# Two mixers of a second block rearranged: queries and keys of retention turned during the projection, retention's units first in the stream, and VectorE adding up the scores of the key selection

## The reference

```
x = x + 0.5 * swiglu(rmsnorm(x), ...)                 # ffn 1
p_a, p_b, p_c = split(rmsnorm(x) @ w_in)              # 1280, 1096 and 1024 columns
x = x + concat([rwkv7(p_a), dsa(p_b), retention(p_c)]) @ w_out
x = x + 0.5 * swiglu(rmsnorm(x), ...)                 # ffn 2
```

```
# rwkv7 (6 heads of 64): w = -softplus(-(w0 + tanh(w_lo) @ w2)) - 0.5; a = sigmoid(a0 + a_lo @ a2); g = sigmoid(g_lo) @ g2
#   decay = exp(-exp(w)); the recurrence uses products of decays within chunks of 64 steps; then a norm per head, times g
# dsa: score[q, s] = sum over 8 heads of iw[q, h] * relu(iq[q, h] . ik[s]); hidden where s > q
#   the 128 best keys of each query are selected; 6 heads of softmax attention on the latent c over the selected keys
# retention (4 heads of 64):
qh, kh = rotate(q), rotate(k)        # rotate: [z1*cos - z2*sin, z1*sin + z2*cos], z1 and z2 the halves of a head
y = (qh @ kh^T * decay(query - key)) @ v;  y = y * rsqrt(mean(y*y) + eps);  out = silu(g) * y
```

## Time and profile before

| | us |
|---|---|
| median of 3 runs | 4016.59 (4015.89 to 4021.63) |
| the profiled execution | 4007.51 |
| its span | 4005.7 |
| TensorE busy | 3738.7 (93%) |
| VectorE busy | 2057.2 (51%) |
| ScalarE busy | 1394.1 (35%) |
| GpSimd busy | 99.6 (2%) |

### The profile page before, as it was taken

How to read it: one execution, slowest core, us unless ns; L and a number is a source line. 1 busy time by engine, 2 the same in 40 slices (tenths; PEclk the granted TensorE clock), 3 DMA queues, 4 the chain that set the end, 5 groups by cost and what they waited for, 6 DMA issues and landing times. The chain is left out here.

```text
span 4005.7 us, 62023 instructions
## 1 busy us (share of the span) xinstructions
PE 3738.7 (93%) x26656; PEld 3221.2 (80%) x26656; DVE 2057.2 (51%) x3299; ACT 1394.1 (35%) x2153; POOL 99.6 (2%) x107
## 2 busy tenths in 40 slices
PE   8989998899889997999997799999999997799998
PEld 8989998788789996888876568888888875658886
DVE  6756654344366635443357554444443347655443
ACT  6534332455343323232225233223232225333321
POOL 0000000000000000000003000000000003100000
PEclk9999999999899998999987899999999997989999
DMA  3222232222122232333310013233233310012332
GB/s 137 68 85 85 90 94 65 71 64 65 48 75 89 89 88 72 96 97 97 96 45 2 22 58 100 95 94 101 95 98 96 96 56 2 23 48 95 100 92 76
DMA packets 87424, 307.03 MB, mean 77 GB/s; under 512 B 9696, under 2 KB 9824, under 8 KB 86896
## 3 DMA queue, kind: packets, MB, share of 16 engines
q1 hardware_dynamic: 87152, 303.08, 24.0%
HBM read 300.91 MB, written 2.13 MB: 76 GB/s over the span
## 5 line engine op out<-in xcount | busy, mean ns | idle before, releaser
L602 DVE TENSOR_TENSOR two_w_lo<-two_raw,two_w_hi 128x1024 fp32r<-128x1024 f32 (+1 forms) x344 | 412.7, 1200 | 848.3 <-ACT two_w_hi L593 845.3
L617 PE MATMUL psum<-two_x_hi,two_w_hi 128*128 128x512 f32 x1856 | 726.0, 391 | 28.4 <-DVE two_w_lo L602 28.4
L617 PE MATMUL psum<-two_x_lo,two_w_hi 128*128 128x512 f32 x1856 | 723.3, 390 | 0.0
L617 PE MATMUL psum<-two_x_hi,two_w_lo 128*128 128x512 f32 x1856 | 723.2, 390 | 0.0
L593 ACT CAST two_w_hi<-two_raw 128x1024 fp32r<-128x1024 f32 (+1 forms) x344 | 352.6, 1026 | 893.1 <-PE psum L617 888.2
L617 PEld LDWEIGHTS psum<-two_x_hi,two_w_hi 128*128 128x128 f32 x1856 | 349.1, 188 | 103.0 <-DVE two_w_lo L602 29.1
L1394 PE MATMUL psum<-one_x_hi,one_w_hi 128*128 128x264 f32 x1408 | 402.1, 286 | 23.1 <-DVE one_x_lo L1538 21.1
L617 PEld LDWEIGHTS psum<-two_x_lo,two_w_hi 128*128 128x128 f32 x1856 | 349.1, 188 | 74.0 <-issue 1.4
L617 PEld LDWEIGHTS psum<-two_x_hi,two_w_lo 128*128 128x128 f32 x1856 | 349.1, 188 | 72.3
L1394 PE MATMUL psum<-one_x_lo,one_w_hi 128*128 128x264 f32 x1408 | 401.0, 285 | 0.0
L1394 PE MATMUL psum<-one_x_hi,one_w_lo 128*128 128x264 f32 x1408 | 400.6, 285 | 0.0
(11 more groups left out here) (411 smaller groups left out, 6594.1 us busy)
## 6 DMA issues: line engine op xcount, KB each, us to landing
two_raw<-in_swi_in SPq DMA_DIRECT2D x176, 512.0 KB, 3.7
one_raw<-in_ffn_in SPq DMA_DIRECT2D x88, 512.0 KB, 3.6
two_raw<-in_swi_out SPq DMA_DIRECT2D x64, 448.0 KB, 3.3
two_raw<-in_mix_in SPq DMA_DIRECT2D x56, 512.0 KB, 3.7
one_raw<-in_attn_w SPq DMA_DIRECT2D x32, 512.0 KB, 3.8
two_raw<-in_swi_out SPq DMA_DIRECT2D x32, 512.0 KB, 3.5
one_raw<-in_ffn_out SPq DMA_DIRECT2D x32, 448.0 KB, 3.3
one_raw<-in_lru_w SPq DMA_DIRECT2D x24, 512.0 KB, 3.6
```

What stands on the lines that cost most here:

```text
L602: self.nc.vector.tensor_tensor(self.m.ws.lo[:, u % self.SLOTS, w], self.m.raw[:, u % self.RAW, w], self.m.ws.hi[:, u % self.SLOTS, w].bitc ...
L617: last = self.nc.tensor.matmul(self.m.ps[:, bank, :], a[:, u % self.SLOTS, w], b[:, k0 + k, :], start=(start and k == 0 and q == 0), stop= ...
```

## The change

- Projection: the sine (with its sign) and cosine tables are loaded into `m.keys` by one more DMA on SP's queue, ahead of the projection's first unit. At units 17 to 20 ScalarE copies one tile of retention's queries or keys with the 32-partition quarters exchanged, four copies a tile. At units 19 to 22 VectorE multiplies that copy by sine, the tile by cosine, and adds.
- Preparation: VectorE adds the scores up, with the head's weight in one instruction each; ScalarE keeps only relu, GpSimd sets the sums to zero and hides later keys beforehand. Tanh becomes a sigmoid with a VectorE instruction behind it. The constant of the log decay goes into the exponentials' scale, and the exponential of the previous step's sum is read from the other one, shifted by a step. Twelve of the 24 scores are placed among the tiles, the first four of them ahead of all, and the sums of squares go behind the third low-rank product. The other twelve scores are added four at a time after each tile of the last pass.
- The mixers' end: no turning. The stream has retention's first six units in front, inside the head; then ten pairs; then 14 key-selection units. RWKV's outputs are made at key-selection units 4, 6 and 8, the norm of retention's output at 11, 13 and 15, and two of the three last products at units 22 and 23. The constants are 128x2048 (1024 KB) instead of 128x3200 (1600 KB).

```diff
-    def load_all(self, sp, preloaded=0):
+    def load_all(self, sp, preloaded=0, ahead_of=None, other=None):
...
+            if u == ahead_of:
+                other()
             sp.dma_start(self.m.raw[:, u % self.RAW, 0:self.cols(u)], self.units[u]).then_inc(
...
+            def turn_constants():
+                sp.dma_start(m.keys[:, 0:2 * SEQ], d["ret_turn"]).then_inc(s["turn_loaded"], 16)
+            if parts[-1].kind == "mix_in":
+                st.load_all(sp, 0, parts[-1].u, turn_constants)
...
+                        if TURN <= v < TURN + 4:
+                            i = v - TURN
+                            act.wait_ge(s["emptied"], 9 + i + 1)
+                            for q in range(4):
+                                ins = nc.scalar.copy(swapped[i][32 * q:32 * q + 32, :],
+                                                     m.other[32 * (q ^ 1):32 * (q ^ 1) + 32, 9 + i, :])
+                            ins.then_inc(s["moved"], 1)
...
+                        if TURN + 2 <= v < TURN + 6:
+                            i = v - TURN - 2
+                            z = m.other[:, 9 + i, :]
+                            dve.wait_ge(s["turn_loaded"], 16)
+                            dve.wait_ge(s["moved"], i + 1)
+                            own.then(nc.vector.tensor_tensor(swapped[i], swapped[i], sin, ALU.mult))
+                            own.then(nc.vector.tensor_tensor(z, z, cos, ALU.mult))
+                            own.wait()
+                            nc.vector.tensor_tensor(z, z, swapped[i], ALU.add).then_inc(s["turned"], 1)
...
@@ rwkv_prepare_stage, TensorE
+            for u in range(FIRST):
+                score(u)
+            pe.wait_ge(s["iw_ready"], 1)
...
+            low_ranks(0)
+            for u in range(4, 6):
+                score(u)
+            low_ranks(1)
+            for u in range(6, 8):
+                score(u)
+            low_ranks(2)
+            pe.wait_ge(s["sq_ready"], C)
+            pe.wait_ge(s["rel_out"], FIRST)
...
+            last.then_inc(s["ss_psum"], 1)
+            for u in range(8, 12):
+                score(u)
...
@@ rwkv_prepare_stage, ScalarE and GpSimd
-                nc.scalar.activation(rel, rel, ACT.Copy, scale=ix.iw[:, b * IH + h:b * IH + h + 1]).then_inc(
-                    s["relu_ready"], 1)
...
-                nc.scalar.activation(w.prev[:, c, :], w.prev[:, c, :], ACT.Exp)
...
-                        nc.gpsimd.tensor_tensor(score, score, rel, ALU.add).then_inc(s["relu_used"], 1)
...
+                nc.gpsimd.memset(score, 0.0).then_inc(s["hidden"], 1)
...
@@ rwkv_prepare_stage, VectorE
+            def add(u):
+                i, h = heads[u]
+                b = blocks[i]
+                n = (b + 1) * QB
+                dve.wait_ge(s["rel_out"], u + 1)
+                if h:
+                    dve.wait_ge(s["added"], u)
+                else:
+                    dve.wait_ge(s["hidden"], 2 * i + 2)
+                nc.vector.scalar_tensor_tensor(ix.score[b], ix.relu[h % 4][:, 0:n], ix.iw[:, b * IH + h:b * IH + h + 1],
+                                               ix.score[b], ALU.mult, ALU.add).then_inc(s["added"], 1)
...
-                own.then(nc.vector.tensor_scalar(L, L, -math.exp(-0.5), None, ALU.mult))
...
-                nc.vector.tensor_tensor(w.prev[:, c, :], cum, L, ALU.subtract).then_inc(s["cum_ready"], 1)
...
+                for u in range(12 + 4 * c, 16 + 4 * c):
+                    add(u)
...
@@ mixers_end_stage
-    LEAD, NORMED = 5, 7
-    stream = [("dsa", a) for a in range(LEAD)]
-    for g in range(NR):
-        stream += [("dsa", LEAD + g), ("ret", g)]
-    stream += [("dsa", a) for a in range(LEAD + NR, NA)]
+    R0 = 6
+    stream = [("ret", r) for r in range(R0)]
+    for g in range(NR - R0):
+        stream += [("dsa", g), ("ret", R0 + g)]
+    stream += [("dsa", a) for a in range(NR - R0, NA)]
...
+    HALF_RET, ALL_RET = NR // 2 - R0, NR - R0
+    RET_SUMS, RET_FIRST, RET_SECOND = ALL_RET + 1, ALL_RET + 3, ALL_RET + 5
+    RWKV_OUT = (4, 6, 8)
...
-                if u < 4:
-                    turn(u)
-                elif u == RET_SUMS:
+                if u == RET_SUMS:
...
+                elif u == RET_FIRST:
+                    pe.wait_ge(s["y_factor"], 1)
+                    spread(m.ps[:, 7, :], e.y_factor[:, 0:2 * NT]).then_inc(s["y_spread"], 1)
+                elif u == RET_SECOND:
+                    pe.wait_ge(s["y_normed"], 1)
+                    spread(m.ps[:, 7, :], e.y_factor[:, 2 * NT:4 * NT]).then_inc(s["y_spread"], 1)
+                elif u == NA - 2:
+                    pe.wait_ge(s["y_normed"], 2)
+                    pe.wait_ge(s["out_ready"], NA - 4)
+                    finish(0, 7)
+                elif u == NA - 1:
+                    pe.wait_ge(s["evicted"], N)
+                    pe.wait_ge(s["out_ready"], NA - 2)
+                    finish(1, 0)
```

More of the change, by code:

```diff
@@ L1594 @@
 TOPK = 128
-RET_COLS = 2 * SEQ + P + 4 * SEQ
+RET_COLS = 4 * SEQ
 HIDDEN = -3.0e38
 TAKEN = -3.4e38
+DECAY = -math.exp(-0.5)
 class Select:
@@ L1690, in rwkv_prepare_stage @@
     heads = [(i, h) for i in range(3) for h in range(IH)]
-    early = ((0, 2), (2, 6), (6, 10))
+    FIRST = 4
+    place = lambda u: 4 + u if u < FIRST else 6 + heads[u][1] % 2
     NT = SEQ // P
@@ L1840, in _ @@
             own.then(nc.vector.memset(m.reset.rearrange("p (n c) -> p n c", c=HD)[:, :, 0:1], 0.0))
+            dve.wait_ge(s["iw_ready"], 1)
+            for u in range(FIRST):
+                add(u)
             for c in range(C):
@@ L1866, in _ @@
                     s["prod_ready"], 1)
+                if c < C - 1:
+                    add(4 + 2 * c)
+                    add(5 + 2 * c)
+            dve.wait_ge(s["ss_psum"], 1)
+            own.then(nc.vector.tensor_scalar(inverse, m.ps[:, 4, 0:2 * NT * C], 1e-24, None, ALU.max))
+            own.wait()
+            nc.vector.reciprocal(inverse, inverse).then_inc(s["ss_ready"], 1)
+            for u in range(8, 12):
+                add(u)
             for c in range(C):
@@ L2323, in mixers_end_stage @@
     c_lat = m.other[:, 3, :]
-    z = [m.other[:, 9 + i, :] for i in range(4)]
-    q, k = z[0:2], z[2:4]
+    q, k = [[m.other[:, 9 + 2 * j + i, :] for i in range(2)] for j in range(2)]
     gate = [m.other[:, 13 + i, :] for i in range(2)]
@@ L2432, in weigh, with finish @@
                                  e.st[u % 4][:, 0:SEQ - j * P], start=(j == 0), stop=(j == NK - 1)).then_inc(s["weighed"], 1)
+            def finish(pair, bank):
+                for h in (2 * pair, 2 * pair + 1):
+                    last = nc.tensor.matmul(m.ps[half(h), bank, :], e.down[:, h * HD:(h + 1) * HD], e.olat[:, h, :],
+                                            start=True, stop=True)
+                last.then_inc(s["final_psum"], 1)
             for c in range(C):
-                nc.tensor.matmul(m.ps[:, bank(c), :], m.head_ones, w.v[:, c, :], start=True, stop=True).then_inc(
+                nc.tensor.matmul(m.ps[:, 2 + c, :], m.head_ones, w.v[:, c, :], start=True, stop=True).then_inc(
                     s["mean_psum"], 1)
+            for i in range(SB):
+                score(i)
             pe.wait_ge(s["c_squared"], 1)
@@ L2462, in _ @@
             last.then_inc(s["c_psum"], 1)
+            pe.wait_ge(s["f_factor"], 1)
             pe.wait_ge(s["q_out"], H)
-            for i in range(SB):
-                score(i)
+            for c in range(C):
+                spread(m.ps[:, 2 + c, :], e.factor[:, 2 * NT * c:2 * NT * (c + 1)]).then_inc(s["spread"], 1)
+            for i in range(3, R0):
+                weigh(i)
+                score(i + SB)
             for i, (kind, u) in enumerate(stream):
-                if i and i + SB - 1 < N:
+                if i < R0:
+                    continue
+                if i > R0 and i + SB - 1 < N:
                     score(i + SB - 1)
                 if kind == "ret":
-                    weigh(i, u)
+                    weigh(i)
                     continue
@@ L2708, in retention_constants @@
     ang = np.tile(ang, (4, 1)).astype(np.float64)
-    turn = np.zeros((P, P), f32)
-    for r in range(P):
-        turn[(r + 32 if r % 64 < 32 else r - 32), r] = -1.0 if r % 64 < 32 else 1.0
+    sign = np.where(np.arange(P) % HD < HD // 2, -1.0, 1.0)[:, None]
     key, query = np.meshgrid(np.arange(P), np.arange(SEQ), indexing="ij")
     decay = [np.where(query >= key, np.exp((query - key) * np.log(1.0 - 2.0 ** (-5.0 - h))), 0.0) * SCALE for h in range(4)]
-    return np.concatenate([np.cos(ang), np.sin(ang), turn] + decay, axis=1).astype(f32)
+    return np.concatenate([np.cos(ang), sign * np.sin(ang)], axis=1).astype(f32), np.concatenate(decay, axis=1).astype(f32)
 def layout(a):
```

271 lines of the change are left out of this document (129 added, 142 removed).

## The result

| kernel | median | lowest to highest | profiled execution | its span | granted clock |
|---|---|---|---|---|---|
| before | 4017.85 us | 4015.89 to 4021.63 (4 runs) | 4007.51 us | 4005.7 us | 0.953 |
| changed | 3966.24 us | 3963.99 to 3967.41 (4 runs) | 3963.99 us | 3962.0 us | 0.961 |

The ratio is 0.9876, 95% interval [0.9862, 0.989]: 51.6 us less between the medians. In the launches beside the experiments the executions of before run from 4002.8 us, with a granted clock of 0.953 as in the profile, to 4025.4 at 0.948.

What follows compares the result with a forecast made beforehand. Most of the program was taken as a weight stream at TensorE's pace (3738.7 of 4005.7 us busy). Mixers' end 2 x 15 plus preparation 2 x 7, projection nothing, gave 44 us: from median 4016.6 to 3972, range 3949 to 3996.

Steps and rivals of the forecast that it cites:

- The end of the mixers: Mixers' end: 83.3 us of TensorE work plus stalls, 94 us against 109.1, a gain of 15 us in each layer.
- RWKV's outputs: Mixers' end: put between key-selection units three times, they stall 1.3 us each, 3.9 in all (bounds 0 and 6).
- root: Mixers' end, unit 11: retention's statistics wait for the root's table load, 2.2 us left (0 to 3.3).
- spreads: Mixers' end, units 13 and 15: VectorE stands until each of two spreads, 1.9 us each, 3.8 (0 to 5).
- rivals A and D: Mixers' stream: A, starts at the lower clock, 3988, 17%; D, TensorE's clock stays low throughout, 4095, 5%.
- Preparation: Preparation stage: ends earlier by 6.8 us, taken as 7 in each layer; bounds 2 and 11.
- I take 5: Preparation: first body (L1870) starts 5 us sooner, from walked 5.6 us in layer 0 and 4.6 in layer 1.
- ScalarE loses 24 weighings and is not late: Preparation: ScalarE, relieved of 24 weighings, was claimed not to be late; no separate size given.
- rival C: Preparation: VectorE replaces GpSimd as last, additions wait; gain 2 us a layer, total -34, 3982; 12%.
- E: Projection: VectorE overruns and holds TensorE, four units by 2 us in each layer, leaving -28, 3988; 3%.
- a wait on the constants in the head: Mixers' end, head: named sign of being wrong; landing no sooner than before would lose 1.6 us a layer.
- Rival B: Mixers' end: stalls vanish as VectorE's lead swallows RWKV's outputs and spreads, 8 us a layer more, -60, 3956; 16%.

Runs made afterwards that it cites:

- s_later: Changed kernel with VectorE's root inversion and multiplications of retention's output one key-selection unit later (12, 14, 16, not 11, 13, 15): 3960.43 us.
- turn_only: Changed kernel's projection and preparation, queries and keys turned beside the projection, but the mixers' end in the order of before: 3972.52 us.
- p_root: Changed kernel with ScalarE's root in preparation ahead of clearing scores 8 to 11, spreads before scores 10 and 11: 3965.88 us.
- t_none: Changed kernel with the turn left out of the projection (no transfer, copies, multiplications or additions for it): 3966.84 us.
- c_more: Changed kernel with constants landing later in the mixers' end (half the table loaded and waited for, then the whole): 3981.98 us, one run.
- s_rwkv: Changed kernel with RWKV's nine output instructions one in each of key-selection units 2 to 10, not three in units 4, 6, 8: 3967.27 us.
- combo: Changed kernel with the edits of s_later, s_rwkv and p_root, scores 10 and 11 behind the first bonus: 3952.80 us.
- fill: combo plus ten TensorE products that nobody reads, behind the last seven scores of preparation: 3951.53 us.

## Why the prediction was right, and where its steps were off

The time fell in the stated range, 6 us below the forecast. That the profiled spans differ by 43.7 us where 44 was forecast is luck in part: preparation gave 3.25 us less than forecast, and the recurrences, in neither my sum nor any rival, 2.70 more. The medians differ by 51.6.

**The end of the mixers** was right in its sum, 94 against 94.12 (95.56 in layer 1), and near in its terms. Measured in layer 0, behind the forecast: RWKV's outputs 0.58 + 1.14 + 1.43 = 3.15 (3.9); 128-key units 0.72 (0.6); root 0.99 (2.2); spreads 1.68 + 1.47 = 3.15 (3.8). Waits on other data add 0.6, and 1.7 us pass between TensorE's end and the next stage (tail 1.4). Together 10.3 of stalls (11.9), beside 83.64 busy (82.4). The head is 24.45 (23 to 24). The stall moved to where I put it, units 11, 13 and 15, and s_later shows its cause: VectorE standing for a result that depends on TensorE's place in the stream. I had the root too dear: its table load of 1.28 us, at 2301.24, runs while TensorE makes a score and a product. And the price of RWKV's outputs came out near for no good reason. I took it from a stretch where TensorE was busy 10.15 of 10.20 us at 0.54, so TensorE hardly stood there and the pairs were long by the clock; the waits now measured are another thing, at 1.00.

**The reason for the gain's size** needs a correction. I wrote that it is less than 19.8 us because the turns' TensorE work was cheap and retention's units must still be done. turn_only shows the turn by itself giving 12.9 and 9.8 us, four fifths and two thirds of each layer's gain, by shortening a unit from 4.8 to 0.8 us and by lifting the clock of RWKV's outputs from 0.54 to 1.00. The order added the smaller part; which of its steps did (retention's units in the head, or its norm in the stream), no run separates.

**The clock** (rivals A and D): 1.00 in the whole of layer 0's stream, and below it only in some 4 us of layer 1's, so A and D are out. But I took the clock as a property of a stage. In the thirteen traces of this study stretches of some 3.5 to 7 us near 1.2 GHz (and one of 14) come and go in the same code, and recurrences, whose code is the same in all of them, take between 104.5 and 110.6 us. The 3.44 us of layer 0's recurrence go, at least in part, with such a stretch, in neither my sum nor any rival. They nearly fill the gap that preparation left.

**Preparation** is the term that was off: 10.75 and not 14. The step that failed is "I take 5" for the first body: it came 3.3 and 2.4 us sooner. With it fails "ScalarE loses 24 weighings and is not late": I had walked TensorE's and VectorE's lists and not ScalarE's, where the root stands behind clearings 8 to 11, and with the root ahead of them the body came 5.0 and 3.1 us sooner still (p_root). The other half held: from the first body to the last addition 25.2 us were forecast, and it is 2112.14 to 2137.34, the same; the wait for the thirteenth score 2.25 (2.2); and VectorE's products on two SBUF operands take 0.69 with GpSimd silent, where L1876 took 1.48. Between rival C (2 a layer) and the forecast (7), 5.4 is nearer to the forecast.

**The projection** cost nothing, as said (E is out by t_none), and the arithmetic held closely: 2.10 idle and three instructions that add 1.80, since each begins a little before the one ahead has ended, leave 0.30.

**The constants** landed 5.9 us after layer 1's stage began (5.4 forecast), and end VectorE's wait of 0.90 us there. That is the sign of being wrong that I named, a wait on the constants in the head; but TensorE waits for nothing in that head after its start, so they are just not the bound. That a landing as late as before, at 7.1, would cost 1.6 us a layer, no run tests: c_more, landing at 9.4 and 9.3 us, lost 1.9 and 6.8, the larger with the low clock.

**The table load.** ScalarE's rows above have the root 1.29 us behind the start of its table load, and the exponentials 1.30 behind theirs. The Trainium skill, page "ScalarE: Activation LUTs", section "What ACT_TABLE_LOAD costs", has about 1283 ns for the load, which agrees, and 1380 ns of draining on top, which these rows don't have. The total that I worked out from it, 5.6 us above the forecast, didn't come. (The page's advice to do all roots together stands in another of its sections, "Table sets: the hidden batching unit".)

Rival B (stalls vanish) was wrong for this kernel but right as an aim: with VectorE's steps one unit later and RWKV's outputs spread, 8.0 us of waits for a division became 1.8.

## What to carry to other kernels

Before pricing a ring of three engines, find the one link in it that isn't part of the unit's own work; moving that link out can be worth most of the ring (here 4.8 us a unit became 0.8). When a statistic or a broadcast by TensorE is put into a stream, let the engine that consumes it do so a unit later than TensorE makes it. Walk the instruction list of every engine to a moved step, the idle engine's too: an in-order list with a wait ahead of it delays as surely as a full one.

## What the runs showed of the hardware

- One wait of 2.05 us on TensorE was followed by 14 us near 1.2 GHz with TensorE busy 13.37 of them (c_more, layer 1), in a stage 6.8 us longer. In layer 0 the same edit made a wait of 0.9 us and a stage 1.9 us longer.
- What p_root and s_rwkv took out (3.7 us of preparation; 6.2 us of TensorE's waits) did not show in their medians, and their traces have more stretches near the low clock; joined with s_later's edit they do show.
- Stages of unchanged code differ from trace to trace: the recurrence by up to 6 us, the changed preparation of layer 1 by 1.7. Two recurrences with the same mean clock, 0.95, took 105.9 and 108.5 us (combo), so the clock isn't all of it.
- Ten products kept TensorE's clock at 1.00 until it ran out of work in preparation; after 3.85 us of idling at the change of stages the recurrence began at 0.50 (fill), as it did without them.
- Three VectorE instructions of 0.69 us beside a weight unit left 0.30 us of slack in 5.44 and cost nothing (27 splits in 141.67 us in the changed kernel, in t_none and in before).
